# The order of two jobs of VectorE in the attention loop: normalising a result, and making the low parts of a prepared piece

## The chip, the cores and the metric

The kernel runs on one core of one Trainium2 chip. The metric is the time of one execution on the device, in microseconds (us); the figure of a kernel is the median of its runs. TensorE does the matrix products, VectorE, ScalarE and GpSimd the rest, and SyncE issues most of the DMA transfers. An engine does its instructions in the order of the program, and a semaphore is how one waits for another.

## The reference

One step of a decoder layer for a prompt of 1024 positions and for 8 single sample tokens, 1024 wide. Cut to what matters here, for each head of the prompt:

```python
z = rmsnorm(x, g) @ w_in                       # then q, k, v of each head, q and k normalised per head
sc = einsum('bqhe,bkhe->bhqk', q, k) * scale + bias    # causal; the bias is a decay or a position bias
p = softmax(sc)
o = einsum('bhqk,bkhe->bqhe', p, v)
```

There are four heads of forgetting attention (A), four of cross-attention into 256 memory tokens (M), and four of dilated attention (C). Each sample token attends to 4096 cached keys and values, which lie in pages that a table names (A), and to smaller caches (C, M). The outputs go through a norm and `w_out`, and then comes a ConvFFN with `w_up` and `w_down`.

## The kernel before

Products are made nearly exact by splitting an operand into a high part (a rounded copy, type fp32r) and a low part (the value less its high part). There are three stages one after the other: the projections, the attention loop, and the output projection with the ConvFFN.

**The attention loop** has 80 steps `g`, `H, s = divmod(g, 8)`: ten units `H` of eight steps. `H` 0 to 3 are the heads of A, 4 and 5 are M (two heads at a time), 6 to 9 are C. In A and C a step makes 128 queries against all the keys before them, and the query tiles alternate between long and short (`ALTERNATE = [7, 0, 6, 1, 5, 2, 4, 3]`): an even step has 8, 7, 6 or 5 blocks of 128 keys, an odd step 1, 2, 3 or 4. In M each step has 4 blocks. H = 9 takes the tiles from 7 down to 0. The loop is unrolled by hand on each engine, and the order of an engine's calls in a step is the order of its queue.

- **TensorE**, step g: `tp(g-2)`, the transposes of the weights of softmax (L1098, L1103); `prep`, the transposes of a piece of q or k of the next unit into bank 3 of PSUM (L983); `qk(g)`, the scores (L1082, L1083, in M L1089, L1090); `v_sum`, a product for the sample tokens (L1139) that uses a 512 KB gather of cached values; `pv_(g-3)`, weights times values (L1116, in M L1120).
- **ScalarE**, step g: a copy of transposed weights (`eva`, L1532), `hi` (the high part of a prepared piece), `ex(g)` (the exponentials, L1521).
- **VectorE**, step g: `evb(g-2)`, the copy of transposed weights beyond four blocks (L2198, even steps of A and C); `score(g)`, scores out of PSUM with the bias and their maximum (L2185, in M L2190); `lo`, the low part of the piece that TensorE transposed one step earlier (L2146 or L2150 for a unit of A or C, two of L2136 or L2140 for a unit of M); `k_mul` in odd steps to g = 31 (L1902) and `k_sum` in the step behind (L1910), which make the samples' scores out of a 512 KB tile of cached keys; `out(g-3)`, a reciprocal (L2207, in M L2214) and the product that writes the normalised result to `oN` (L2210, in M L2217); then the odd jobs, among them `cm_dot` (L2227 and L2229).

**The pieces.** A unit of A or C is prepared in four pieces, at steps s = 0, 2, 4, 6 of the unit ahead of it, a unit of M in three, at s = 0, 3, 6. VectorE makes the low part one step later, so for A and C in odd steps. From g = 3 on there are 33 steps with `lo`: 27 for a unit of A or C, 6 for one of M.

**Who waits for what.** `out(g-3)` waits for `pv_(g-3)`, which TensorE issues last in its own step g. `pv_(g-3)` waits for `out(g-4)`, since all results use the same bank:

```python
def pv_(g):
    ...
    T_.wait("s_o", g)            # out(g - 1) is done with bank 6
def prep(H, piece):
    ...
    T_.wait("p_lo", PN[(H, piece)] - 1)      # the piece before has left bank 3
def out(g):
    T_.wait("s_pv", g + 1)
```

`score(g)` waits for `qk(g)`, `qk(g)` for `score(g-2)`, `tp(g)` for `ex(g)`. SyncE loads key tiles by `k_load`, each when `k_sum` has freed its slot, and at its step 29, behind one of these, it loads `qdil` (1 MB, into a part of `oN`), for which the first `cm_dot`, at g = 35, waits.

Of the kernel before, what the change touches and what calls it, by code (L numbers as in the profile page):

```python
# [98 lines left out]
def build(nc, t):  # L99
# [5 lines left out]
    with ctx:  # L105
# [205 lines left out]
        def S(name):  # L311
            if name not in sems:
                sems[name] = ctx.enter_context(nc.semaphore(name))
            return sems[name]
# [160 lines left out]
        def two(H):  # L475
            return HEADS[H][0] != MEMG

        def prep_piece(H, s):

            if H + 1 >= len(HEADS):  # L480
                return None
            return (PREP_TWO if two(H + 1) else PREP_MEM).get(s)
# [8 lines left out]
        def qtile(g):  # L491
            H, s = divmod(g, NT)
            return s if not two(H) else ALTERNATE[s] if H + 1 < len(HEADS) else NT - 1 - s
# [32 lines left out]
        def k_total(n):  # L526
            return 64 * (n // 4 + 1) if n < NKA else 64 * (NKA // 4) + 16 * ((n - NKA) // 4 + 1)
# [1289 lines left out]
        def _(dve):  # L1817
# [81 lines left out]
            def k_mul(n):  # L1899

                kv = ring[:, n % 4]
                dve.tensor_tensor(kv, kv, qb[:, n // 8:n // 8 + 1, :].broadcast_to([P, 4, WG]), ALU.mult).then_inc(S("dve_chain"), 1)  # L1902
                chain[0] += 1
                multiplied[n] = chain[0]

            def k_sum(n):

                kv = ring[:, n % 4]
                out = sA[:, n // 8, 4 * (n % 8):4 * (n % 8) + 4, :]
                dve.tensor_reduce(out=out, in_=kv.rearrange("p g (h e) -> p (g h) e", e=HD), axis=AX.X, op=ALU.add)\  # L1910
                    .then_inc(S("k_used"), 1)
# [93 lines left out]
            def column_max(i):  # L2005

                grp, a, b, bank_, c0 = GMAX[i]
                T_.wait("mx_pe", 2 * i + 1)
                link(dve.tensor_reduce(out=mx[0:b - a], in_=ps[0:b - a, bank_, c0:c0 + P], axis=AX.X, op=ALU.max))
                dve.tensor_scalar(mxb[0:b - a, :], ones[0:b - a, :], mx[0:b - a], None, ALU.mult).then_inc(S("mx"), 1)  # L2010
# [158 lines left out]
            def score(g):  # L2169

                H, s = divmod(g, NT)
                grp, hh = HEADS[H]
                W = P * nblk(g)
                T_.wait("s_qk", g + 1)
                if two(H):
                    if grp == ATT:
                        T_.wait("toeA_ld", 16)
                        bias_ = toeA[:, 0:W][:, ::-1]
                    else:
                        T_.wait(f"toeC_ld{hh % 2}", 16 * (hh // 2 + 1))  # L2180
                        bias_ = toeC[:, hh % 2, 0:W][:, ::-1]
                    if g >= 2:
                        T_.wait("s_tpa", g - 1)
                        T_.wait("s_tpb", big_to[g - 1])
                    dve.tensor_tensor_reduce(out=lg[:, g % 2, 0:W], in0=SBANK(g % 2)[:, 0:W], in1=bias_, scale=-1.0,  # L2185
                                             scalar=3.0e38, op0=ALU.add, op1=ALU.min, accum_out=nm[:, g % 2, 0:1])\
                        .then_inc(S("s_nm"), 1)
                else:
                    T_.wait("s_exp", g - 1)
                    dve.tensor_reduce(out=nm[:, g % 2, 1:3], in_=SBANK(g % 2)[:, 0:W].rearrange("p (a c) -> p a c", a=2), axis=AX.X,  # L2190
                                      op=ALU.max, negate=True).then_inc(S("s_nm"), 1)

            def evb(g):
                nb = nblk(g)
                if nb > 4:
                    T_.wait("s_tpb", big_to[g + 1])
                    T_.wait("s_pv", g - 1)
                    dve.tensor_copy(pts[:, g % 2, 4:nb, :].rearrange("p b c -> p (b c)"),  # L2198
                                    ps[:, 5, 0:(nb - 4) * P]).then_inc(S("s_evb"), 1)

            def out(g):
                grp, hh = HEADS[g // NT]
                T_.wait("s_pv", g + 1)
                col = OCOL[grp] + hh * HD
                if two(g // NT):
                    one, o0 = ((0, 1), (HD, 0))[(g // NT) % 2]
                    dve.reciprocal(rc[:, g % 2, 0:1], ps[:, 6, one:one + 1]).then_inc(S("dve_chain"), 1)  # L2207
                    chain[0] += 1
                    T_.wait("dve_chain", chain[0])
                    dve.tensor_scalar(oN[:, qtile(g), col:col + HD], ps[:, 6, o0:o0 + HD], rc[:, g % 2, 0:1],  # L2210
                                      None, ALU.mult).then_inc(S("s_o"), 1)
                else:
                    z = ps[:, 6, 1:1 + 2 * HD].rearrange("p (a e) -> p a e", a=2)
                    dve.reciprocal(rc[:, g % 2, :], ps[:, 6, 0:2 * HD + 2:2 * HD + 1]).then_inc(S("dve_chain"), 1)  # L2214
                    chain[0] += 1
                    T_.wait("dve_chain", chain[0])
                    dve.tensor_tensor(oN[:, qtile(g), col:col + 2 * HD].rearrange("p (a e) -> p a e", a=2), z,  # L2217
                                      rc[:, g % 2, :].unsqueeze(2).broadcast_to([P, 2, HD]), ALU.mult).then_inc(S("s_o"), 1)
# [91 lines left out]
            for g in range(STEPS + 3):  # L2310
                H, s = divmod(g, NT)
                if 0 <= g - 2 < STEPS:
                    evb(g - 2)
                if g < STEPS:
                    score(g)
                piece = prep_piece(*divmod(g - 1, NT)) if g else None
                if piece:
                    lo((g - 1) // NT + 1, piece)
                if g in K_STEP:
                    n = K_STEP[g]  # L2320
                    T_.wait(f"ring_ld{n % 4}", k_total(n))
                    k_mul(n)
                if g - 1 in K_STEP:
                    n = K_STEP[g - 1]
                    T_.wait("dve_chain", multiplied[n])
                    k_sum(n)
                if g >= 3:
                    out(g - 3)
                if g in TURN_MAX:
                    column_max(TURN_MAX[g])  # L2330
                if g in SEND_MAX:
                    max_copy(SEND_MAX[g])
                if g == 2:
                    subtract_a(0)
                if g == 32:
                    forget_bias(1)
                    maxima(0, 4, 8)
                if g == 35:
                    subtract_a(1)
                    new_weight(0)  # L2340
                if g in CMK_AT:
                    cm_dot(CMK_AT[g])
                if g == 45:
                    dil_bias()
                    new_key(1)
                    maxima(1, 0, 8)
                if g == 56:
                    T_.wait("k_used", NKA + NCM)
                    maxima(2, 0, 8)
                if g == 48:  # L2350
                    subtract_cm(1)
                    new_weight(1)
                if g == 60:
                    subtract_cm(2)
                if g == 54:
                    key_sums(0)
                if g == 55:
                    key_sums(1)
                if g == 63:
                    key_sums(2)  # L2360
                if g in (56, 57):
                    w_out(g - 56)
                if g == 59:
                    sample_gate()
                if 68 <= g < 76:
                    scale_early(g - 68)
                if g == STEPS - 3:
                    T_.wait("samp_pe", 1)
                    dve.tensor_copy(small[0:8, :, 148:152], ps[0:8, 7, 0:24].rearrange("p (g h) -> p g h", h=8)[:, :, 0:NH])\
                        .then_inc(S("den_cp"), 1)  # L2370
                if g == 75:
                    T_.wait("s_pv", 8 * NT)
                    w_out_lo(0)
                if g == STEPS - 2:
                    for x in range(2):
                        scale_last(x)
                if STEPS < g:
                    turn_lo(g - STEPS - 1)
# [461 lines left out]
```

## Time and profile before

| | |
|---|---|
| median of 3 runs | 1390.29 us (1386.17 to 1390.61) |
| the profiled execution, its time / its span | 1387.22 / 1385.5 us |
| busy over the span: TensorE, its weight loads | 1320.2 us (95%), 1208.8 us (87%) |
| busy over the span: VectorE, ScalarE, GpSimd | 960.5 (69%), 550.7 (40%), 250.7 us (18%) |
| mean granted clock of TensorE, share of full speed | 0.978 |
| HBM traffic over the span | 144 GB/s |

Busy time is that of instructions that work; waits are idle time. A granted clock of 1.00 is 2.4 GHz, 0.50 is 1.2 GHz. The attention loop runs from about 300 to 569 us of the span; behind it TensorE has the output projection and the ConvFFN to do, which take the rest.

### The profile page before, as it was taken

The numbers are of one execution on the slowest core, as the hardware profiler recorded it, in microseconds if no ns is written. First come the engines' busy times: TensorE is split into PE (matmuls) and PEld (weight loads), VectorE is DVE, ScalarE is ACT, GpSimd is POOL, SyncE is SP. The second block draws the span as 40 slices with busy tenths as digits, with TensorE's granted clock in tenths as the row PEclk, the third lists the DMA queues.
The fourth block names the chain that finished last, engine by engine and source line by source line (L and its number), as shares of the span: only waits on it lengthen the run. The fifth ranks groups of instructions, "written<-read, shape, count | busy, mean of one in ns | idle before, by whom it ended". The sixth has DMA issues, their size and how long they took to land.

```text
span 1385.5 us, 24359 instructions
## 1 busy us (share of the span) xinstructions
PE 1320.2 (95%) x9293; PEld 1208.8 (87%) x9293; DVE 960.5 (69%) x1391; ACT 550.7 (40%) x908; POOL 250.7 (18%) x242
## 2 busy tenths in 40 slices
PE   6899999989988899899999999999999999999999
PEld 4668788866767677899899999999999999999999
DVE  6848789979987777758868878778878896111111
ACT  6422221146656566543544434543443454100100
POOL 5540013342332251100101111110110100000000
PEclk9799999989998899999999999999999999999999
DMA  8148866669999865432132222222222185322222
GB/s 291 57 133 258 228 194 194 196 190 265 297 293 281 266 223 140 147 123 77 62 107 69 70 92 70 69 93 80 66 85 92 47 305 162 112 75 80 81 73 73
DMA packets 149613, 201.57 MB, mean 145 GB/s; under 512 B 12692, under 2 KB 112556, under 8 KB 149216
## 3 DMA queue, kind: packets, MB, share of 16 engines
q1 hardware_dynamic: 130684, 140.12, 33.1%
q0 software_dynamic: 12848, 46.73, 10.7%
q10 hardware_dynamic: 5964, 13.16, 3.2%
q8 instruction: 74, 1.21, 0.4%
q14 instruction: 43, 0.35, 0.1%
HBM read 169.64 MB, written 29.82 MB: 144 GB/s over the span
## 4 chain that ended last, share of the span: by engine, by line
PE 64%; DVE 14%; DMA 8%; issue 5%; POOL 3%; ACT 2%; ACTq 1%; SPq 1%; DVEq 0%; POOLq 0%
PE ps L1275 8%; PE ps L1276 8%; PE ps L1277 8%; PE ps L1336 5%; PE ps L1337 5%; PE ps L1338 5%; PE ps L1116 3%; PE ps L1015 3%; PE ps L1016 3%; PE ps L1017 3%; DMA upr<-in_w_upL 2%; PE ps L1139 2%; DMA vring<-in_cache_a_v,gtab 2%; DMA oN<-scr_qs 2%; PE ps L1098 2%
## 5 line engine op out<-in xcount | busy, mean ns | idle before, releaser
L1275 PE MATMUL ps<-hhi,uph 128*128 128x258 f32 x704 | 200.8, 285 | 4.5 <-issue 1.4
L1276 PE MATMUL ps<-hlo,uph 128*128 128x258 f32 x704 | 199.4, 283 | 0.0
L1277 PE MATMUL ps<-hhi,upl 128*128 128x258 f32 x704 | 199.1, 283 | 0.0
L1015 PE MATMUL ps<-whi,hhi 128*128 128x512 f32 (+1 forms) x376 | 145.9, 388 | 13.1 <-DVE wlo L1858 9.3
L2580 DVE TENSOR_TENSOR dnl<-dnr,dnh 128x896 fp32r<-128x896 f32 (+2 forms) x24 | 27.2, 1135 | 174.9 <-ACT dnh L1771 174.9
L1017 PE MATMUL ps<-whi,hlo 128*128 128x512 f32 (+1 forms) x376 | 142.7, 379 | 0.0
L1016 PE MATMUL ps<-wlo,hhi 128*128 128x512 f32 (+1 forms) x376 | 142.6, 379 | 0.0
L1275 PEld LDWEIGHTS ps<-hhi,uph 128*128 128x128 f32 x704 | 133.8, 190 | 6.4 <-DVE ug L2538 2.5
L1276 PEld LDWEIGHTS ps<-hlo,uph 128*128 128x128 f32 x704 | 134.0, 190 | 0.0
L1277 PEld LDWEIGHTS ps<-hhi,upl 128*128 128x128 f32 x704 | 133.6, 190 | 0.0
L2765 POOL TENSOR_TENSOR upr<-upr 128x512 f32<-128x512 f32 x22 | 30.3, 1375 | 450.3 <-DMA upr<-in_w_upL 373.7
L1336 PE MATMUL ps<-fh,dnh 128*128 128x344 f32 x336 | 107.5, 320 | 1.6 <-DVE dnl L2580 1.6
L1337 PE MATMUL ps<-fl,dnh 128*128 128x344 f32 x336 | 107.8, 321 | 0.0
L1338 PE MATMUL ps<-fh,dnl 128*128 128x344 f32 x336 | 107.2, 319 | 0.0
L1771 ACT ACTIVATE dnh<-dnr 128x896 fp32r<-128x896 f32 (+2 forms) x24 | 23.7, 987 | 192.8 <-DMA dnr<-in_w_down 192.8
L1015 PEld LDWEIGHTS ps<-whi,hhi 128*128 128x128 f32 x376 | 72.4, 193 | 31.0 <-DVE wlo L1858 12.6
L1116 PEld LDWEIGHTS ps<-vst,pts 128*128 128x128 f32 x576 | 69.4, 191 | 31.5 <-issue 27.5
L1655 ACT ACTIVATE uph<-upr 128x1024 fp32r<-128x1024 f32 (+1 forms) x66 | 79.3, 1203 | 40.6 <-DMA upr<-in_w_upL 38.0
L2467 DVE TENSOR_TENSOR upl<-upr,uph 128x1024 fp32r<-128x1024 f32 (+1 forms) x66 | 92.1, 1395 | 0.4 <-ACT uph L1655 0.3
L2730 POOL DMA_INDIRECT vring<-in_cache_a_v,gtab x64 | 63.5, 992 | 144.9 <-PE ps L1139 140.9
L1116 PE MATMUL ps<-vst,pts 128*128 128x65 f32 x576 | 76.3, 278 | 9.4 <-DVE oN L2210 6.6
L1017 PEld LDWEIGHTS ps<-whi,hlo 128*128 128x128 f32 x376 | 72.4, 192 | 13.9
(339 smaller groups left out, 3600.2 us busy)
## 6 DMA issues: line engine op xcount, KB each, us to landing
upr<-in_w_upL SPq DMA_DIRECT2D x88, 256.0 KB, 3.4
ring<-in_cache_a_k SPq DMA_DIRECT2D x168, 128.0 KB
scr_act<-va SPq DMA_DIRECT2D x22, 516.0 KB, 2.6
ring<-in_cache_a_k ACTq DMA_DIRECT2D x88, 128.0 KB
wst<-in_w_in SPq DMA_DIRECT2D x32, 256.0 KB, 3.7
fr<-scr_act SPq DMA_DIRECT2D x14, 516.0 KB, 5.5
dnr<-in_w_down SPq DMA_DIRECT2D x12, 448.0 KB, 3.9
dnr<-in_w_down SPq DMA_DIRECT2D x10, 512.0 KB, 4.0
```

Source lines behind the costliest of these rows:

```text
L1015: pe.matmul(out, lh, whi[:, sl, 0:w], start=(kc == 0), stop=False)
L1016: pe.matmul(out, lh, wlo[:, sl, 0:w], start=False, stop=False)
L1017: i = pe.matmul(out, ll, whi[:, sl, 0:w], start=False, stop=(kc == KC - 1))
L1116: i = pe.matmul(ps[:, 6, 0:HD + 1], pts[:, g % 2, j, :], vst[:, hp % 2, j, VCOL[H % 2]], start=(j == 0), stop=(j == nb - 1))
L1275: pe.matmul(out, hi_, r_hi[:, cs], start=(first and i == 0), stop=False, skip_group_check=not first)
L1276: pe.matmul(out, hi_, r_lo[:, cs], start=False, stop=False, skip_group_check=not first)
L1277: m = pe.matmul(out, lo_, r_hi[:, cs], start=False, stop=(i == 3), skip_group_check=not first)
L1336: pe.matmul(out, hi_, a_hi[:, cs], start=first, stop=False)
L1337: pe.matmul(out, hi_, a_lo[:, cs], start=False, stop=False)
L1338: m = pe.matmul(out, lo_, a_hi[:, cs], start=False, stop=last)
L1655: act.activation(uph[p % 2][:, a:b, :], upr[p % 2][:, a:b, :], ACT.Copy).then_inc(S("st_hi"), 1)
L2467: dve.tensor_tensor(upl[p % 2][:, a:b, :], upr[p % 2][:, a:b, :], uph[p % 2][:, a:b, :].bitcast(f32), ALU.subtract).then_inc(S("st_lo"), 1)
```

## The change

In a step that has a low part to make, VectorE calls `out(g-3)` straight behind `score(g)`, ahead of `lo` and so ahead of `k_mul` and `k_sum` too. In the other steps `out` stays where it was. No instruction is added or taken away.

```diff
                 if g < STEPS:
                     score(g)
                 piece = prep_piece(*divmod(g - 1, NT)) if g else None
+                if piece and g >= 3:
+                    out(g - 3)
                 if piece:
                     lo((g - 1) // NT + 1, piece)
                 if g in K_STEP:
                     n = K_STEP[g]
                     T_.wait(f"ring_ld{n % 4}", k_total(n))
                     k_mul(n)
                 if g - 1 in K_STEP:
                     n = K_STEP[g - 1]
                     T_.wait("dve_chain", multiplied[n])
                     k_sum(n)
-                if g >= 3:
+                if g >= 3 and not piece:
                     out(g - 3)
```

## Rows read from the trace of the kernel before

**Rows 1.** Windows: us, busy (count) PE, PEld, DVE, ACT, POOL, clock, DMA share, GB/s.
```profile
306.00:394.00 88.00, 80.52 (x701) 61.45 (x699) 78.83 (x169) 52.22 (x87) 28.05 (x27) 0.99 1.04 285
...
416.00:466.00 50.00, 42.65 (x306) 34.84 (x305) 37.55 (x77) 30.44 (x78) 8.85 (x10) 0.78 0.89 285
466.00:570.00 104.00, 98.22 (x891) 76.44 (x887) 78.17 (x201) 65.51 (x139) 33.31 (x39) 0.99 0.60 185
570.00:1385.50 815.50, 801.91 (x5930) 797.08 (x5930) 509.11 (x558) 292.48 (x394) 70.56 (x62) 1.00 0.29 96
```

**Rows 2.** Groups by line, 310 to 566 us: busy, mean ns | idle before.
```profile
L1116 PE MATMUL ps<-vst,pts 128*128 128x65 f32 x566 | 75.0, 278 | 8.7 <-DVE oN L2210 5.9 <-issue 2.2
...
L2146 DVE SCALAR_TENSOR_TENSOR qhl<-ps,ssx,qhl 64x512 fp32r<-64x512 f32 x14 | 10.5, 751 | 0.5
...
L2150 DVE TENSOR_TENSOR klc<-ps,khh 64x512 fp32r<-64x512 f32 x13 | 8.9, 685 | 0.2
```

**Rows 3.** VectorE in time, steps g = 8 to 10: start, us, instruction.
```profile
329.75 0.28 DVE L2210 TENSOR_SCALAR oN<-ps,rc 128x64 f32<-128x64 f32 x1
329.95 0.28 DVE L2185 CUSTOM_DVE_ANT_0 lg<-ps,toeA 128x128 f32<-128x128 f32 x1
...
330.16 0.68 DVE L2150 TENSOR_TENSOR klc<-ps,khh 64x512 fp32r<-64x512 f32 x1
330.76 1.21 DVE L1902 TENSOR_TENSOR ring<-ring,qb 128x1024 f32<-128x1024 f32 x1
331.89 0.15 DVE L2207 RECIPROCAL rc<-ps 128x1 f32<-128x1 f32 x1
332.08 0.28 DVE L2210 TENSOR_SCALAR oN<-ps,rc 128x64 f32<-128x64 f32 x1
332.40 0.69 DVE L2198 COPY pts<-ps 128x512 f32<-128x512 f32 x1
333.65 1.09 DVE L2185 CUSTOM_DVE_ANT_0 lg<-ps,toeA 128x896 f32<-128x896 f32 x1 [0.56 <-PE ps L1083]
```

**Rows 4.** TensorE in time, `pv_` of steps 9 and 11.
```profile
330.18 1.30 PE L1116 MATMUL ps<-vst,pts 128*128 128x65 f32 x10 [0.43 <-DVE oN L2210]
...
336.42 1.97 PE L1116 MATMUL ps<-vst,pts 128*128 128x65 f32 x16 [0.33 <-DVE oN L2210]
```

**Rows 5.** VectorE in time, steps 28 and 30.
```profile
390.81 1.51 DVE L2136 SCALAR_TENSOR_TENSOR qhl<-ps,ssx,qhl 64x512 fp32r<-64x512 f32 x2
...
397.76 0.83 DVE L2185 CUSTOM_DVE_ANT_0 lg<-ps,toeA 128x640 f32<-128x640 f32 x1 [0.65 <-PE ps L1083]
```

**Rows 6.** TensorE in time: its three long waits, and `pv_` at full clock.
```profile
394.24 1.75 PE L1116 MATMUL ps<-vst,pts 128*128 128x65 f32 x14 [2.49 <-DVE oN L2210]
...
421.28 1.97 PE L1120 MATMUL ps<-vst,pts 128*128 128x65 f32 x8 [3.57 <-DVE oN L2217]
...
435.03 1.10 PE L1120 MATMUL ps<-vst,pts 128*128 128x65 f32 x8
...
454.94 0.40 PE L1195 MATMUL ps<-ca,small 128*32 128x128 f32 x1 [2.31 <-DVEq L2003]
```

**Rows 7.** VectorE in time, steps 36 to 39.
```profile
420.94 0.29 DVE L2217 TENSOR_TENSOR oN<-ps,rc 128x128 f32<-128x128 f32 x1
...
431.06 0.69 DVE L2190 TENSOR_REDUCE nm<-ps 128x2 f32<-128x512 f32 x1 [3.11 <-PE ps L1090]
```

**Rows 8.** Windows: TensorE's clock (third from the end) behind two waits.
```profile
392.00:396.00 4.00, 1.76 (x16) 1.79 (x17) 3.60 (x7) 0.63 (x2) 0.95 (x1) 1.00 1.07 277
...
424.00:428.00 4.00, 4.00 (x25) 3.48 (x27) 3.19 (x5) 3.17 (x7) 0.00 (x0) 0.50 0.97 265
```

**Rows 9.** The chain that ended last: the load of `qdil`.
```profile
393.99 22.03 DMA oN<-scr_qs
```

**Rows 10.** VectorE in time, step 61 of head group C.
```profile
512.22 0.17 DVE L2207 RECIPROCAL rc<-ps 128x1 f32<-128x1 f32 x1 [1.34 <-PE ps L1116]
```

**Rows 11.** TensorE in time, `prep` of step 62.
```profile
512.68 0.60 PE L983 MATMUL ps<-ca,qst 128*128 128x128 f32 x4
```

## The prediction

> **What bounds the kernel now.** I read the page first (busy shares and the 40 slices), then the windows by stage, the groups by line in the attention loop, the three engines' instructions in time through the loop, and the chain that ended last. The windows give the shares [rows 1]: from 570 us on TensorE is busy 801.9 of 815.5 us, and the change has no instruction there, so whatever the loop gains or loses arrives whole at the end. The loop has three stretches. In the first, 306 to 394 us, VectorE is busy 78.8 of 88.0 us and TensorE 80.5: neither has room, and the DMA share is 1.04. In the second the granted clock averages 0.78, which is a mix of the full 2.4 GHz and 1.2 GHz. In the third TensorE is busy 98.2 of 104 us, VectorE 78.2.
>
> The instructions in time say how the two engines hang together in the first stretch. In an odd step the queue of VectorE has `score` (0.28 us long at g = 9), `lo`, `k_mul`, then `out` [rows 3]. The `pv_` for which that `out` waits started at 330.18, just behind the end at 330.03 of the `out` of the step before, and took 1.30 us [rows 4]. So `pv_` starts with `score`, and `lo` and `k_mul` (2 us together) fill the time in which it runs: by the time they end, at 331.97, the product is done and `out` goes at once. That is the fact on which I build. The `pv_` of an odd step belongs to an even, long tile: 8, 7, 6 or 5 blocks, 1.97 us for 8 and 1.30 for 5 [rows 4].
>
> **What could be gained.** An earlier `out` frees bank 6 for the next `pv_`. Over the 256 us of the loop the products of A and C waited 5.9 us for `out` [rows 2], most of it behind even steps, whose `out` the change doesn't move; the two waits of 0.43 and 0.33 us at steps 9 and 11 are of this kind [rows 4]. In an odd step the next `pv_` on TensorE comes only after transposes, a piece, long scores and a `v_sum`; it doesn't wait for the `out` that is moved. Two long waits are different, and I cost them below.
>
> **The change, first stretch.** It adds and removes no instruction. At g = 9 `out` now waits for the end of `pv_` at 331.48. From the rows: 0.05 us from there to the reciprocal, 0.39 until the next instruction (start to start), `lo` 0.60, `k_mul` 1.13, `evb` 0.64, all start to start. The next `score` can start at 331.48 + 2.81 = 334.29, and it started at 333.65 [rows 3]. The shift is 0.64 us, less than the 1.24 us of new idle time, since VectorE had waited 0.56 us for the scores there and that wait is swallowed. TensorE isn't the later of the two: its next piece began at 332.20 and now waits for `lo` until 332.5, which puts the end of its scores, 333.62, at 334.0. The next even step has `score`, `k_sum`, `out` without a gap, and the next `pv_` hangs on that `out`, so each shift is kept. The same sum for the odd steps g = 5 to 25 (11 steps, the `pv_` 1.97 to 1.30 us long, `lo` 0.60 or 0.78) gives 0.59 to 0.96 us each, and 1.25 at g = 25, where no wait for scores is there to swallow: together 8.9 us. At g = 3 `pv_` is long done, and nothing is lost. Bounds: nothing, if another resource sets the pace (below), and 11 times 1.24, so 13.6 us, if no old wait swallows anything.
>
> **Steps 28 and 31.** Step 28 is even, and its piece is two instructions, 1.51 us [rows 5]. Its `out` has a one-block `pv_` long done and stood behind `lo` and `k_sum`: 2.7 us. TensorE waited 2.49 us for it [rows 6]. Moved, it lets TensorE go on at 391.8 instead of 394.24, and `score` of step 30, which waited for TensorE until 397.76 [rows 5], starts when VectorE is ready, at 396.4: 1.4 us gained. Step 31 is odd again, 0.9 us lost. Together -0.5.
>
> **Second stretch, M.** Step 36: `out` ended at 421.23 behind a `lo` of 1.5 us [rows 7], and TensorE sat idle 3.57 us, to 421.28 [rows 6]. Moved, `out` ends at 419.6 and the idle time is 2.0 us. Behind that wait the clock was 0.50 [rows 8]; eight instructions of `pv_` took 1.97 us there and 1.10 at full clock [rows 6], a ratio of 0.56. VectorE waited 3.11 us at step 39 for scores of this slow time [rows 7]. The end of my bounds where the clock still falls is the earlier start alone, -1.5. If it stays up, the 9.8 us from 421.28 to 431.06 take 9.8 x 0.56 = 5.5: -4.3 (the 1.5 isn't added, since the `score` of step 37 stands behind `lo` as before). Which one? The nearest rows are a wait of 2.49 us behind which the clock stayed at full level, and one of 2.31 us behind which it fell (the mean of 0.78 has both drops in it) [rows 1, 6, 8]. The new wait is shorter than either; I take -4.3.
> The Trainium skill, "TensorE: Matmul & The Clock Gate", section "What's actually happening", says that the halved clock is the default and that activity lifts it. By that rule a shorter idle time favours the full clock, a sum of +9.9; if the clock fell nevertheless, the sum would be +12.7.
> Steps 41, 43 and 45 have `cm_dot` behind `out`, so a `lo` of 0.6 to 0.75 us now lies in front of it that had been done while `pv_` ran: +0.6, +0.4, +0.8. Steps 33 and 39 cancel to about 0.1. Without the clock: +1.9.
>
> **The 1 MB load** took 22.03 us and landed just as VectorE came to it [rows 9]. Its issue stands behind `k_sum` of step 28, 0.4 us later than before against the rest, and its user comes 0.5 us earlier: a wait of 0 to 1 us. I take 0, as the transfers have more time per step.
>
> **Third stretch, C.** Steps 49, 51 and 53 have `cm_dot` too, and VectorE sets the pace: +0.6, +0.6, +0.4. From step 57 on TensorE does. At 61 `out` came at 512.22, waiting 1.34 us for `pv_` with `lo` already done [rows 10]; now `lo` (0.74 us) starts at 512.63 and ends at 513.4, and the next `prep`, which began at 512.68 [rows 11], waits: +0.7. The same at 63 and 69: +0.9, +0.7. At 65 and 67 a `v_sum` behind `pv_` covers it, at 55, 57 and 59 `pv_` is done or `prep` is late anyway: 0. Together +3.9.
>
> **Sum.** 8.9 - 0.5 + 1.9 - 4.3 + 3.9 = +9.9 us on the 1387.2 us of the profiled execution: 1397.1. That execution is 3.1 us below the median of the runs, so I forecast 1400.
>
> **Rivals.**
> 1. As forecast, but the clock falls behind step 36 as before: +12.7, 1403. For it: the fall behind 2.31 us [rows 6]. Chance 0.22; the forecast has 0.42.
> 2. New idle time makes the clock fall once more elsewhere: one fall cost 4.3 us, so 1407. Against it: the new gaps are 0.4 to 1.1 us of TensorE at a time. Chance 0.08.
> 3. Not slower: the transfers set the pace of the first stretch. The DMA share is 1.04 there [rows 1]. If the gathers and key tiles let no step go sooner, the stalls of VectorE fall into time that it would have waited anyway: the 8.9 go, and what stays is +1.0, 1391. It decides where the shift per pair of steps, 0.6 to 1.0 us, is below the wait for a transfer; but before, neither engine waits more than some tenths for one, in few steps. A part of it (half of the 8.9) gives 1395.5. Chance 0.18 for both.
> 4. Faster: the pace of the first stretch is the transfers' as in rival 3, and the clock stays up behind the 2.31 us wait too, which takes another 4.3: 1.0 - 4.3 = -3.3, 1387, and 1385 if the stalls of the third stretch are swallowed by half. It decides where both falls of the clock go and the first stretch costs nothing. Chance 0.04.
> What is left, 0.06, is no change within the measurement for reasons that I don't see.
> The Trainium skill, the same page, section "Architectural detail: the array is 16× 32×32, not 1× 128×128", calls VectorE's queue a strict FIFO. By that rule nothing passes the waiting `out`, which is what the stall in the first sum is made of; a queue that let `lo` pass would give no shift at all, 1390.
>
> **Range and chances.** What a measurement here can tell from no change is about 0.3%, 4.2 us. Low end: half of the first term, less one us: 1394. High end: one more fall of the clock: 1407. Slower by over 0.3% (above 1394.5): the forecast, rivals 1 and 2, and part of 3: 0.80. Within: 0.15. Faster: 0.05.
>
> **What the profile after would show.** The reciprocals of odd steps wait 0.7 to 1.6 us for L1116 in the first stretch, where they hardly did; `lo` and `k_mul` start behind L2210; a unit of A takes 28 us instead of 25; VectorE's waits for L1083 shrink. The 2.49 us wait is gone, and the 3.57 is 2.0. At steps 62, 64 and 70 `prep` waits for `lo`. Each busy total stays. I am wrong if `pv_` of odd steps starts earlier than the `out` ahead of it ends, if scores wait for the gathers, or if the clock has another pattern than assumed.

## The result, and the profile after

| | before | after |
|---|---|---|
| median of the runs beside each other | 1390.45 us (6 runs, 1386.17 to 1395.60) | 1415.78 us (6 runs, 1412.59 to 1422.85) |
| the profiled execution, its time / its span | 1387.22 / 1385.5 us | 1415.53 / 1413.7 us |
| mean granted clock of TensorE | 0.978 | 0.967 |

The ratio is 1.0202, 95% interval 1.0179 to 1.0226: the change makes the kernel 2.0% slower. By this ratio it is some 28 us, as between the two profiled spans (28.2); the two medians of the table lie 25.3 us apart. The forecast was +9.9 us, and its range ended at 1407. The direction was right, and the size is over two and a half times what I forecast.

The page of the kernel after: busy us (share) xinstructions, and the granted clock in 40 slices.

```profile
PE 1336.2 (95%) x9293; PEld 1218.3 (86%) x9293; DVE 962.9 (68%) x1391; ACT 550.8 (39%) x908; POOL 248.7 (18%) x242
...
PEclk9799999989987899999999999999999999999999
```

VectorE's work is the same, 962.9 us against 960.5. TensorE's instructions are the same too, but its busy time grew by 16.0 us, 1320.2 to 1336.2: the same products took longer, at a lower clock. That is the first sign that idle time of VectorE isn't the whole story.

The windows by stage of the kernel after (clock third from the end); the bounds are those of [rows 1], moved with the work.

```profile
306.00:404.00 98.00, 83.70 (x716) 62.71 (x714) 77.83 (x168) 52.02 (x87) 25.58 (x27) 0.99 1.02 265
404.00:428.00 24.00, 21.24 (x152) 16.44 (x151) 17.64 (x39) 11.88 (x23) 5.69 (x6) 0.79 1.05 331
428.00:482.00 54.00, 45.03 (x307) 36.02 (x305) 38.30 (x78) 30.74 (x79) 8.52 (x9) 0.78 0.67 216
482.00:594.00 112.00, 103.93 (x906) 78.87 (x905) 78.75 (x206) 66.16 (x139) 34.58 (x38) 0.95 0.56 172
```

The first stretch takes about 98 us instead of 88, at the same clock of 0.99. In the others the clock tells more. A mean of 0.78 over 54 us that is a mix of 1.00 and 0.50 is 54 x 0.22 x 2 = 23.8 us at half speed; with the other two windows (24 x 0.21 x 2 and 112 x 0.05 x 2) the loop after 404 us has 45 us at 1.2 GHz. The same sum over [rows 1] gives 22 + 2 = 24 us before.

**Step 9, where I worked the sum out.** VectorE in time, kernel after: start, us, instruction, and in brackets the idle time before it.

```profile
332.03 0.28 DVE L2185 CUSTOM_DVE_ANT_0 lg<-ps,toeA 128x128 f32<-128x128 f32 x1
...
333.60 0.17 DVE L2207 RECIPROCAL rc<-ps 128x1 f32<-128x1 f32 x1 [1.28 <-PE ps L1116]
333.80 0.28 DVE L2210 TENSOR_SCALAR oN<-ps,rc 128x64 f32<-128x64 f32 x1
334.00 0.67 DVE L2150 TENSOR_TENSOR klc<-ps,khh 64x512 fp32r<-64x512 f32 x1
334.60 1.21 DVE L1902 TENSOR_TENSOR ring<-ring,qb 128x1024 f32<-128x1024 f32 x1
335.73 0.68 DVE L2198 COPY pts<-ps 128x512 f32<-128x512 f32 x1
336.33 1.07 DVE L2185 CUSTOM_DVE_ANT_0 lg<-ps,toeA 128x896 f32<-128x896 f32 x1
```

From `score` of step 9 to `score` of step 10 it is now 336.33 - 332.03 = 4.30 us; it was 333.65 - 329.95 = 3.70 [rows 3]. The shift is 0.60 us, and the forecast for this step was 0.64. The reciprocal waits 1.28 us for the product, then `lo` and `k_mul` come, and the wait for scores is gone.

**Where the time came.** The start of each `score(g)`, read in the two traces, after less before, in us:

| g | 5 | 8 | 14 | 20 | 26 | 30 | 32 | 35 | 38 | 41 | 46 | 49 | 56 | 64 | 79 |
|---|---|---|---|---|---|---|---|---|---|---|---|---|---|---|---|
| shift | -0.17 | 2.09 | 4.35 | 7.12 | 10.67 | 9.18 | 10.37 | 13.78 | 12.36 | 16.05 | 18.76 | 18.05 | 22.20 | 24.11 | 25.32 |

Here it stands beside the forecast, with the steps grouped as there:

| | forecast | measured |
|---|---|---|
| ahead of g = 5 | 0 | -0.2 |
| first stretch, g = 5 to 26 | +8.9 | +10.8 |
| steps 28 to 48 (28 and 31: -0.5, 36: -4.3, M steps: +1.9) | -2.9 | +7.4 |
| from g = 49 to the end of the loop | +3.9 | +7.3 |
| behind the loop | 0 | +2.9 |
| sum | +9.9 | +28.2 |

Most of the miss is in the line of steps 28 to 48, 10.3 us of 18. TensorE in time, kernel after: its waits over 1.5 us from step 31 on, and two close together at step 53.

```profile
413.18 0.41 PE L983 MATMUL ps<-ca,kst 128*128 128x128 f32 x2 [1.67 <-DVE q1c L2136]
...
433.38 1.26 PE L1120 MATMUL ps<-vst,pts 128*128 128x65 f32 x8 [1.91 <-DVE oN L2217]
...
447.19 0.63 PE L983 MATMUL ps<-ca,kst 128*128 128x128 f32 x4 [1.78 <-DVE q1c L2136]
...
473.70 0.28 PE L1195 MATMUL ps<-ca,small 128*32 128x128 f32 x1 [2.06 <-DVEq L2003]
...
500.77 1.75 PE L1116 MATMUL ps<-vst,pts 128*128 128x65 f32 x14 [0.94 <-DVE oN L2210]
503.32 1.04 PE L1139 MATMUL ps<-vring,sA 128*4 128x256 f32 x8 [0.80 <-ACT mkd L1540]
```

The stretch behind each of these waits (the last two together) in windows of 4 us, kernel after; the clock is third from the end.

```profile
416.00:420.00 4.00, 4.00 (x23) 2.92 (x23) 3.28 (x7) 0.68 (x2) 1.75 (x3) 0.50 1.19 262
437.00:441.00 4.00, 4.00 (x27) 3.23 (x29) 2.49 (x5) 2.95 (x7) 0.00 (x0) 0.50 0.33 91
450.00:454.00 4.00, 4.00 (x23) 2.95 (x22) 1.42 (x4) 1.93 (x6) 0.77 (x1) 0.50 0.85 241
478.00:482.00 4.00, 4.00 (x17) 3.46 (x15) 1.27 (x3) 1.78 (x3) 0.00 (x0) 0.50 0.54 135
504.00:508.00 4.00, 4.00 (x22) 3.30 (x22) 2.85 (x4) 1.86 (x3) 1.26 (x1) 0.50 0.42 126
```

Behind all of them the clock stands at 0.50, 1.2 GHz. Two of these five falls were there before, behind waits of 3.57 us (now 1.91) and 2.31 us (now 2.06) [rows 6]. Three weren't in the profile before: `prep` at step 32 waits 1.67 us and at step 40 1.78 us, both for `lo` of a memory unit, and at step 53 two waits come close together. The third may not be of the change: runs 1, 4, 10 and 12 below have the old order at step 53, waits of 0.83 to 0.85 and about 0.80 us there, and a fall behind them. The kernel before has these two waits too (0.85 and 0.80 us) and stayed at 1.00. The `lo` that `prep` waits for at step 32 is this one; VectorE in time, kernel after, step 31.

```profile
411.00 0.17 DVE L2207 RECIPROCAL rc<-ps 128x1 f32<-128x1 f32 x1 [1.10 <-PE ps L1116]
411.20 0.28 DVE L2210 TENSOR_SCALAR oN<-ps,rc 128x64 f32<-128x64 f32 x1
411.52 1.51 DVE L2136 SCALAR_TENSOR_TENSOR q1c<-ps,ssx,q1c 64x512 fp32r<-64x512 f32 x2
```

In step 31 VectorE first waits for the product of a long tile, and then makes a double low part of 1.51 us, not a single one of 0.7. TensorE has nothing to do until it is made.

### The profile page after: what moved, and what is told of

Its sections match the earlier page's. It is cut to its first block, busy times and chain, and to the rows that moved or that the text cites. A ratio compares the mean times of both kernels' runs of the same rounds, so it can differ in the third digit from the quotient of the medians.

```text
span 1413.7 us, 24359 instructions
## 1 busy us (share of the span) xinstructions
PE 1336.2 (95%) x9293; PEld 1218.3 (86%) x9293; DVE 962.9 (68%) x1391; ACT 550.8 (39%) x908; POOL 248.7 (18%) x242
## 4 chain that ended last, share of the span: by engine, by line
PE 65%; DVE 17%; issue 5%; DMA 5%; POOL 3%; ACT 2%; ACTq 2%; SPq 1%; DVEq 0%; POOLq 0%
PE ps L1275 8%; PE ps L1276 8%; PE ps L1277 8%; PE ps L1336 5%; PE ps L1337 5%; PE ps L1338 5%; PE ps L1116 4%; PE ps L1015 3%; PE ps L1016 3%; PE ps L1017 3%; DMA upr<-in_w_upL 2%; PE ps L1139 2%; DVE ring L1902 1%; DVE lg L2185 1%; DVE sA L1910 1%
```

## The experiments

Each was timed against the kernel before on the same chip. "Shift" is the start of `score` less that of the kernel before, in the profiled executions. It is counted from g = 5 on, since executions differ in the steps ahead of that by up to 4 us whatever was edited: the clock from 310 to 318 us is 1.00 in the kernel before and 0.50 in runs 5 and 9.

**1 to 4. The change in four parts.** Each kernel has the new order in one group of steps alone:

```diff
+                early = bool(piece) and 3 <= g <= 27              # run 1
+                early = bool(piece) and 31 <= g <= 47 and g != 36 # run 2
+                early = bool(piece) and g >= 49                   # run 3
+                early = g in (28, 36)                             # run 4
+                if early:
+                    out(g - 3)
                 if piece:
                     lo((g - 1) // NT + 1, piece)
...
-                if g >= 3:
+                if g >= 3 and not early:
                     out(g - 3)
```

Run 1, the first stretch:

> Normalise first only in the odd steps 3 to 27 (13 steps; 12 of them have a piece), as before everywhere else. Theory (the result waits for its product and holds the low part and k_mul back): the score of step 28 starts 10.7 us later than before, as in the changed kernel, and that is kept to the end: +11 us, 1401. Rival A (most of the 25 us is halved clock, the stalls themselves are given back later): under +5. Rival B (transfers absorb it once the rest is as before): under +5, with new waits for gathers.

Run 2, the M steps and 31 without 36:

> Normalise first only in steps 31, 33, 39, 41, 43, 45 and 47. Theory (the next piece on TensorE waits for the late low part, the clock falls behind that wait, and everything in the fall takes nearly twice as long): +9 to +10 us, of which 2 to 4 are stalls of VectorE and the rest are two more falls of the clock than before, behind steps 31 and 39. Rival (the falls come from the slower pace ahead, not from these waits): +2 to +4 and the two falls of before.

Run 3, head group C:

> Normalise first only in the steps from 49 on. Theory (stalls of 0.5 to 1 us at steps 49, 51, 53, 61, 63 and 69, and a fall of the clock behind step 53): +5 to +7 us at the end of the loop. Rival (TensorE is the bound here and hides it): under +3.

Run 4, the two steps where a gain was forecast:

> Normalise first only in steps 28 and 36, where the product is done long before. Theory (TensorE no longer waits 2.5 and 3.6 us for the result): -1.4 at step 30 and -1.4 at step 38, so -3 us, or -6 if the clock stays up behind step 36. Rival (the steps behind are bound by something else and take it back): no change.

| run | median us | ratio to before (95%) |
|---|---|---|
| 1, first stretch | 1400.57 | 1.0075 (1.0050 to 1.0101) |
| 2, M | 1401.65 | 1.0083 (1.0058 to 1.0107) |
| 3, C | 1396.32 | 1.0040 (1.0019 to 1.0062) |
| 4, steps 28 and 36 | 1389.93 | 0.9996 (0.9981 to 1.0011) |

The four add up to 0.75 + 0.83 + 0.40 - 0.04 = 1.94%, the whole change is 2.02%: the parts hardly act on each other. In us these are 10.4, 11.5, 5.6 and -0.6; the forecast for the same steps was 8.9, 2.8, 3.9 and -5.7. So the timed runs, and not only one profile of each kernel, put the largest miss, 8.7 us, in the steps of run 2, and the next, 5.1 us, in steps 28 and 36. (The profiled execution of run 2, 1394.86 us, is the fastest of its six, and that of run 3, 1402.82, the second slowest of its ten.) In run 1 the shift grows from 2.99 at g = 5 to 13.85 at g = 26, +10.9, as in the whole change. In run 2 the shift is 0.2 at g = 30 and 9.4 at the end of the loop, where the forecast for its steps was 0.9 + 1.9 = 2.8: here is the error. TensorE in time, run 2, shows the same two new waits for `lo`, with step 36 left as it was:

```profile
404.21 0.66 PE L983 MATMUL ps<-ca,kst 128*128 128x128 f32 x2 [1.67 <-DVE q1c L2136]
...
424.36 1.97 PE L1120 MATMUL ps<-vst,pts 128*128 128x65 f32 x8 [3.58 <-DVE oN L2217]
437.49 0.66 PE L983 MATMUL ps<-ca,kst 128*128 128x128 f32 x4 [1.78 <-DVE q1c L2136]
```

Run 4 was to give the two gains alone, and gave nothing that can be measured. Its profile shows the gain at step 28, -1.4 us (2.94 at g = 28, 1.53 at g = 30), and then a loss of 3.1 at g = 36. VectorE in time and the chain that ended last, run 4:

```profile
421.19 1.23 DVE L2227 TENSOR_TENSOR ring<-ring,oN 128x1024 f32<-128x1024 f32 x1 [3.03 <-DMA oN<-scr_qs]
```

```profile
397.32 23.84 DMA oN<-scr_qs
```

This is the 1 MB load of `qdil`, for which I had taken 0 and bounded 0 to 1 us. It was issued 3.33 us later than in [rows 9] (that execution ran 2.94 us late at step 28, and `k_sum` behind `out` adds 0.4), and took 1.8 us longer, so it landed at 421.16. `score` of step 30 had won 1.4 us back by then, and `cm_dot` waited 3.03 us. The -1.4 of step 36 (5.10 to 3.70) and -1.8 at step 39 came after it, and the sum is nothing. That the early `out` makes this wait isn't shown: run 10 below has no early `out` and waits 3.00 us for the same load, run 12 has it and waits 1.89. In the whole change nothing waits for the load, since its steps take longer there.

**5 and 6. Which of the two jobs that `out` passed costs the time?** The order on VectorE was `out`, `lo`, `k_mul` in the change. Run 5 puts `out` between the two, run 6 puts `lo` last.

```diff
                 if piece:
                     lo((g - 1) // NT + 1, piece)
+                early = bool(piece) and g >= 3              # run 5: lo, out, k_mul / k_sum
+                if early:
+                    out(g - 3)
                 if g in K_STEP:
...
-                if g >= 3:
+                if g >= 3 and not early:
                     out(g - 3)
```

```diff
-                if piece:
+                if piece and g < 3:
                     lo((g - 1) // NT + 1, piece)
                 if g in K_STEP:
...
                 if g >= 3:
                     out(g - 3)
+                if piece and g >= 3:                        # run 6: k_mul / k_sum, out, lo
+                    lo((g - 1) // NT + 1, piece)
```

> In steps with a piece the order is low part, result, k_mul or k_sum: the low part is as early as before, the result is ahead of the multiply alone. Theory (what costs is the late low part everywhere, and the multiply held back in the first stretch): VectorE still fills part of the product's time with the low part, so the first stretch costs 2 to 4 us instead of 10.9; step 28 gives 1.4 or less back; from step 32 on it is the kernel before. 0 to +3 us. Rival (the wait for the product costs the same wherever it stands ahead of other work): +8 or more.

> The order is k_mul or k_sum, result, low part: the multiply fills the product's time, and the low part is the late one, as late as in the changed kernel or later. Theory for the first stretch (VectorE's idle time is the cost, the wait of TensorE for the low part is covered): +2 to +5 us at step 28. From step 31 on the order is that of the changed kernel, with the same late low parts: +12 to +15 at the end of the loop, of both together +15 to +19. Rival (the late low part is the whole cost in the first stretch too): +10 there, +25 in all.

| run | median us | ratio (95%) | shift over the first stretch, g = 5 to 26 |
|---|---|---|---|
| 5, `lo`, `out`, `k_mul` | 1388.11 | 0.9991 (0.9973 to 1.0010) | +1.0 |
| 6, `k_mul`, `out`, `lo` | 1407.00 | 1.0123 (1.0096 to 1.0150) | +8.7 |

Run 6 missed my theory by far. There `out` has `k_mul` ahead of it and hardly waits, so idle time of VectorE for `pv_` can't be the cause, yet the first stretch loses 8.7 us. The waits from 318 to 395 us say what took its place: engine and line, waited for: us, times, longest. First the kernel before:

```profile
DVE lg L2185 <- PE ps L1083: 4.1, 10, 0.6
```

The kernel after:

```profile
DVE rc L2207 <- PE ps L1116: 15.2, 11, 1.8
...
PE ps L983 <- DVE qhl L2146: 4.7, 6, 0.9
...
PE ps L983 <- DVE klc L2150: 1.6, 4, 0.5
```

Run 6:

```profile
DVE lg L2185 <- PE ps L1083: 11.7, 11, 1.4
DVE rc L2207 <- PE ps L1116: 2.3, 5, 0.7
...
PE ps L983 <- DVE qhl L2146: 4.7, 6, 0.9
...
PE ps L983 <- DVE klc L2150: 1.7, 4, 0.5
```

In run 6 `lo` is late, `prep` (L983) waits for it, the scores stand behind `prep` on TensorE, and VectorE waits 11.7 us for the scores. The change has the same waits on TensorE, 6.3 us (6.4 in run 6), hidden behind VectorE's own idle time. So there may be two limits that lie on each other. Runs 9 to 11 take `prep` out of the way to see.

Run 5 is the neutral place: `lo` comes on time, and `k_mul` behind `out` costs only 1.0 us. Over all of the loop it is no change within the measurement.

Run 6 shows one more thing. `prep` at step 32 waits 1.67 us for the double `lo`, as in the kernel after, but in this execution the clock stays up behind the wait (third from the end):

```profile
413.82 0.41 PE L983 MATMUL ps<-ca,kst 128*128 128x128 f32 x2 [1.67 <-DVE q1c L2136]
```

```profile
417.00:421.00 4.00, 3.83 (x38) 2.69 (x39) 3.63 (x9) 1.37 (x4) 1.41 (x2) 1.00 1.17 228
```

Steps 31 to 35 cost 0.35 us there (9.81 to 10.16) and 4.6 in the kernel after. So of what that step costs the wait itself is the small part, and the clock the large one.

**7 and 8. Is it the clock?** In both, TensorE multiplies the identity by itself into an unused part of PSUM where it would wait; nothing reads these products, and the rest is as in the kernel they are added to.

```diff
+            def keep_warm(bank_, n):
+                for _ in range(n):
+                    pe.matmul(ps[:, bank_, 0:P], ident, ident, start=True, stop=True)
...
+                if g in WARM_PREP:                # ahead of prep: run 8, {32: 10, 40: 11}
+                    slot_free(g)
+                    keep_warm(2 * (g % 2), WARM_PREP[g])
...
+                if g in WARM_PV:                  # ahead of pv_: run 7 {37: 20}, run 8 {37: 12}
+                    keep_warm(5, WARM_PV[g])
...
+                if g in WARM_MX:                  # ahead of L1195: run 7 {46: 14}, run 8 {46: 12}
+                    keep_warm(5, WARM_MX[g])
```

Run 7, on the kernel before:

> The kernel before, with 20 and 14 products of the identity (128x128, into bank 5 of PSUM, which nothing uses there; the outputs are the same) on TensorE at step 37 ahead of the product and at step 46 ahead of the transposed maxima, where it sat idle 3.6 and 2.3 us. Theory (the clock falls behind a stretch with little work, and the 10 us at 1.2 GHz behind each cost about 4): no fall behind these two, -4 to -8 us, 1384. Rival (the fall has another cause, or VectorE sets the pace there): no change, or +1 for the products themselves.

Run 8, on the kernel after:

> The changed kernel with 10, 12, 11 and 12 products of the identity on TensorE in its waits at steps 32, 37, 40 and 46 (banks of PSUM that are free there; the outputs are the same). Theory (its three extra falls of the clock in M come from these waits, which the late low part made): the score of step 48 starts 9 to 12 us later than in the kernel before instead of 18, and the whole is 6 to 9 us faster than the changed kernel, 1408. Rival (the falls follow the slower pace in general): as the changed kernel, 1416.

| run | median us | ratio to before (95%) |
|---|---|---|
| 7, before with products in its two long waits | 1382.31 | 0.9944 (0.9922 to 0.9967) |
| 8, after with products in its four | 1398.24 | 1.0067 (1.0035 to 1.0099) |

Windows from 400 to 490 us, in turn before, after, run 7 and run 8; the clock is third from the end.

```profile
400.00:490.00 90.00, 79.62 (x634) 62.71 (x631) 70.19 (x151) 54.35 (x133) 24.45 (x26) 0.87 0.88 273
```

```profile
400.00:490.00 90.00, 77.84 (x553) 60.24 (x555) 63.92 (x138) 48.06 (x113) 18.95 (x20) 0.79 0.77 245
```

```profile
400.00:490.00 90.00, 84.16 (x774) 66.85 (x766) 77.63 (x166) 57.81 (x142) 29.67 (x30) 1.00 0.94 290
```

```profile
400.00:490.00 90.00, 82.27 (x747) 66.53 (x745) 72.99 (x158) 54.97 (x132) 23.69 (x25) 1.00 0.85 275
```

From 404 us on the clock stays at 1.00 in both, and run 8 is 17.5 us faster than the change without the products, where I had expected 6 to 9. Some 8 us of that are the two falls that the kernel before has too, by run 7. (I had counted three extra falls in M; the profile after has two there, at steps 32 and 40.) TensorE in time, run 8, shows what fills the wait at step 32; ten calls are twenty records:

```profile
412.20 2.40 PE L1167 MATMUL ps<-ca 128*128 128x128 f32 x20
414.43 0.38 PE L983 MATMUL ps<-ca,kst 128*128 128x128 f32 x2
```

Now run 8 can be set against run 7, the new order against the old with no fall of the clock from 404 us to the last `score` in either. The difference of their shifts grows by 10.9 us over the first stretch, by 0.3 from g = 26 to 49, and by 5.4 in C (run 8: 0.64, 11.52, 4.73, 10.86 at g = 5, 26, 49, 79; run 7: 0.48, 0.51, -6.57, -5.88). One fall of run 7 lies just ahead, behind its wait for `out` at step 29, where it had no products:

```profile
394.99 1.75 PE L1116 MATMUL ps<-vst,pts 128*128 128x65 f32 x14 [2.49 <-DVE oN L2223]
```

```profile
396.00:400.00 4.00, 4.00 (x29) 3.34 (x28) 1.69 (x5) 1.97 (x3) 0.00 (x0) 0.63 1.03 268
```

It moved run 7 by 1.1 us (0.77 to 1.89, g = 28 to 30), so the 0.3 would be 1.4 without it. The steps from 28 to 48 then cost 0.3 to 1.4 us without the clock, and 6 to 7 of their 7.4 are the clock's; in C 1.9 of the 7.3 are. The timed runs agree: with products in both, the new order costs 1.0067 / 0.9944 = 1.0124, 17 us; the other 11 of the 28 are gone with the products.

**9 to 11. The two limits of the first stretch.** TensorE's `prep` moves behind the scores, so that a late `lo` holds up no score. Run 9 has it on the kernel after, run 10 on the kernel before as a control, run 11 on the order of run 6.

```diff
+                if g < STEPS:
+                    qk(g)
                 if piece:
                     prep(H + 1, piece)
-                if g < STEPS:
-                    qk(g)
```

> The changed kernel with the transposes of the next piece behind the scores on TensorE instead of ahead of them, so that no score waits for a late low part. Theory A (in the first stretch both VectorE's idle time and the late low part are enough by themselves, and each alone costs nearly the whole): still +8 to +10 at step 28 against step 5, and the waits of the piece move behind the scores; in M and C, where only the late low part counts, the extra falls of the clock go or move: 1403 to 1409. Rival B (the late low part is all of it): +1 to +3 in the first stretch and about 1393.

> The kernel before with the same move on TensorE, as the control of the run above. Both theories: within 4 us of the kernel before.

> Order k_mul, result, low part on VectorE, and the transposes of the piece behind the scores on TensorE: VectorE hardly waits and no score waits for the low part. Both theories: the 8.7 us of the same order without the move fall to +1 to +3 in the first stretch. If they stay, the late low part hurts in another way than by holding the scores.

| run | median us | ratio (95%) | shift, g = 5 to 26 |
|---|---|---|---|
| 9, `out`, `lo`, `k_mul`; `prep` late | 1404.85 | 1.0124 (1.0088 to 1.0161) | +10.5 |
| 10, as before; `prep` late | 1390.40 | 1.0008 (0.9980 to 1.0035) | +0.2 |
| 11, `k_mul`, `out`, `lo`; `prep` late | 1400.69 | 1.0077 (1.0054 to 1.0100) | +0.5 |

The waits of run 9 from 318 to 395 us:

```profile
DVE rc L2207 <- PE ps L1116: 15.4, 11, 1.8
```

The control shows that the move itself costs nothing. In the first stretch run 9 has no wait for `lo` among TensorE's products, and it loses 10.5 us all the same: VectorE's idle time alone, 15.4 us in 11 waits, is enough. Run 11 against run 6 shows the other: the same order on VectorE, +0.5 instead of +8.7, so there the loss was only the scores behind a late `prep`. Each limit alone costs 8.7 or 10.5 us, and both together 10.8. Run 11 is slower than before by 0.77% still; in its profile most of that comes in one place, where the shift goes from -3.0 at g = 31 to 5.2 at g = 35. There `k_mul` waited 4.10 us for its tile of cached keys (line 1), so that the double `lo` behind it came late, TensorE waited 5.31 us for it (line 2), and the clock fell. VectorE and TensorE in time, run 11:

```profile
401.80 1.23 DVE L1902 TENSOR_TENSOR ring<-ring,qb 128x1024 f32<-128x1024 f32 x1 [4.10 <-DMA ring<-in_cache_a_k]
...
405.12 0.66 PE L983 MATMUL ps<-ca,kst 128*128 128x128 f32 x2 [5.31 <-DVE q1c L2136]
```

**12. The best of what was seen.** The kernel before with `out` first only at steps 28 and 36, and products at steps 37 (12) and 46 (14).

> The kernel before with normalise first in steps 28 and 36 alone, and 12 and 14 products of the identity on TensorE at steps 37 and 46. Theory (the 1.4 us of step 30 come on top of the clock kept up): -7 to -11 us, 1381. Rival (the earlier result is worth nothing once the clock stays up): as the kernel before with the products, 0.994.

1382.95 us, ratio 0.9945 (0.9918 to 0.9973): the same as run 7. The early `out` adds nothing to it. In its profile `cm_dot` waited 1.9 us for the load of `qdil`, the wait at step 37 outlasted the twelve products by 1.16 us, and the clock fell behind it all the same (0.72 from 424 to 436 us). Run 7 is the simplest version that beats both kernels, by 0.56% and, as 0.9944 / 1.0202, by 2.5%.

## Why the prediction was wrong, point by point

Two steps of it failed. It let a late `lo` cost its own length on VectorE and nothing on TensorE, where the double `lo` of steps 31 and 39 made waits of 1.67 and 1.78 us with a fall of the clock behind them: forecast 2.8 us for the steps of run 2, measured 11.5. And it took the clock to stay up behind step 36, a gain of 4.3 us; with the 1.4 at step 28 that made 5.7, where run 4 measured 0.6.

- **First stretch, 8.9: the mechanism was right, the size low.** It measured 10.8 (10.9 in run 1). At the step that I worked out the shift is 0.60 against 0.64; over the pairs it is 0.6 to 1.3, where I had 0.6 to 1.0 and 1.25 for the last. The wait of TensorE's `prep` for `lo`, of which I had said that it isn't the later of the two, is nearly as late, and by run 6 would cost 8.7 by itself. The bound of 13.6 held.
- **Steps 28 and 31, -0.5.** The gain at 28 was forecast as 1.4, and `score` of step 30 came 1.4 us sooner (10.59 to 9.18). Step 31 was the first error. I priced its `lo` as one of 0.9 us of shift on VectorE, and didn't follow the double `lo` (1.51 us) to the one who waits for it. TensorE's `prep` at step 32 waited 1.67 us, the clock fell, and steps 31 to 35 cost 4.6 us.
- **Step 36, -4.3: this step of the prediction failed.** I held that the clock would stay up behind a wait of 2.0 us, since it had stayed up behind 2.49 us [rows 6]. The wait was 1.91 us, near the 2.0 that I worked out, and the clock fell, as it did behind this wait in all four executions that have it (after, runs 6, 9 and 11). What came was the end of my bounds where it falls: -1.4, against my -1.5. The row that I leaned on was the luck of one execution: the same wait of 2.49 us at step 29 had a fall behind it in runs 1 and 7. The page of the Trainium skill that I named, "TensorE: Matmul & The Clock Gate", section "What's actually happening", says that activity lifts a clock that is otherwise halved; the traces agree as far as runs 7 and 8 go, 1.00 from 400 to 490 us with products in the waits against 0.87 and 0.79 without. My reading of it, that a shorter wait would be safe, was wrong.
- **Rival 2, chance 0.08.** It is what came, at steps 32 and 40 by the new waits, and at step 53, where a fall comes with the old order too. I had argued against it that "the new gaps are 0.4 to 1.1 us of TensorE at a time"; that is true of the pieces for A and C (0.5 to 1.0 us), and false of the two double ones, 1.67 and 1.78. Nor is a gap in that range safe: at step 53 the clock fell behind 0.94 and 0.80 us. A row that I had [rows 5] shows a double `lo`, 1.51 us. Its `prep` was the next thing in TensorE's queue.
- **M steps, +1.9.** With the clock out of it, the steps from 28 to 48 come to +0.3 to +1.4 (run 8 less run 7), where the forecast without the clock is 0.9 - 1.4 - 1.5 + 1.9 = -0.1. With the clock they cost 7.4.
- **C, +3.9.** The clock-free part is 5.4, by run 8 less run 7: 2.4 from g = 49 to 56, where I had 1.6, and 3.1 behind it, where I had 2.3. The shifts at 62, 64 and 70 are there, 0.9, 1.0 and 0.9 for my 0.7, 0.9 and 0.7. The early ones are larger since `prep` waits for `lo` there too, 0.53 us at step 52 and 1.00 at step 56. The other 1.9 is the clock, which fell in step 53; since it falls there with the old order too, it isn't shown that the change made it.
- **Rivals 3 and 4, the transfers.** Wrong: the first stretch took the whole shift with a DMA share of 1.02, and no wait for a transfer appears in its list of waits. But the transfers aren't far off. Where a run keeps the pace of the kernel before through the first stretch, VectorE often waits for one at the end of it: 1.6 to 2.3 us for a key tile at step 27 in runs 2, 4, 7, 10 and 12, 2.02 and 4.10 us for one at step 31 in runs 3 and 11, and for `qdil` in runs 4, 10 and 12. With the slower first stretch (after, runs 1, 6, 8, 9) no such wait appears, nor in the profile of the kernel before.
- **VectorE's queue.** The Trainium skill, the same page, section "Architectural detail: the array is 16× 32×32, not 1× 128×128", calls it a strict FIFO, and the trace after agrees: `lo` starts only behind the reciprocal that waited, at 334.00 behind 333.60.

So of the 28.2 us, 10.9 + 0.3 + 5.4 = 16.6 are waits that VectorE's order makes, and 9.0 are the clock's in the loop (7.4 - 0.3 and 7.3 - 5.4); with the fall of run 7 at step 29 taken out it is 17.7 and 7.9. The timed runs say 17 and 11. The forecast had 12.7 for the first and -2.8 for the second.

**What stays open.** The 2.9 us behind the loop: in the profiles of the twelve experiments this part differs from that of the kernel before by -1.8 to +2.6 us, whatever was edited, so it may be the scatter of one execution; no run tells it apart. Why the clock stays up behind a wait in one execution and falls behind the same wait in another isn't settled either, and with it the share of each fall: in steps 28 to 48, with the old order in all of them, the shift changed by -4.1 us in run 1 and, with the old order to step 48, by +7.0 in run 3.

## What to carry to other kernels

When an instruction is moved back in a queue, ask who on the other engines waits for it and for how long, at every size that it comes in: the longest form of it, not the mean, makes the worst wait. An instruction that waits for a product belongs behind work that fills the time of that product, and a job that feeds another engine belongs ahead of it; the order `lo`, `out`, `k_mul` lost nothing, each of the other two lost over 1%. And where TensorE has to wait 1 to 2 us or more, look at the clock behind the wait, in several executions, and try some products that nobody reads in it.

## What the runs showed of the hardware that I had not expected

The granted clock fell to 0.50 behind waits of TensorE of 1.67, 1.78 and 1.91 us, and stood at 1.00 behind one of 2.49 us [rows 6, 8]; the length of a single wait doesn't decide. Nor does the code: in the profiled executions the same wait is followed by a fall in some and not in others.

| TensorE waits | us | clock fell in | stayed at 1.00 in |
|---|---|---|---|
| step 29, old order at 28 | 2.49, 2.50 | runs 1, 7 | before, run 2 |
| step 32, `lo` late | 1.67 | after, run 2 | run 6 |
| step 37, `out` first at 36 | 1.91 | after, runs 6, 9, 11 | none |
| step 40, `lo` late | 1.78 | after, runs 2, 6 | none |
| step 53, old order | 0.83 to 0.85, 0.80 or 0.81 | runs 1, 4, 10, 12 | before, runs 5, 7 |
| step 53, new order | 0.94, 0.80 | after, runs 3, 6 | run 8 |

Ten to twenty products of the identity in a wait kept it up in runs 7 and 8; in run 12, where the wait outlasted twelve of them, it fell. How long it stays down differs too. Run 1 has the order of the kernel before in all steps from 28 on, and its window from 400 to 490 us reads:

```profile
400.00:490.00 90.00, 77.02 (x647) 62.14 (x647) 71.41 (x155) 54.86 (x131) 22.43 (x24) 0.92 0.90 282
```

0.92 against 0.87, so 90 x 0.08 x 2 = 14 us at half speed against 23, although it holds a third fall, the one behind 2.49 us. In run 3, with the old order up to step 48, VectorE waited 2.02 us for a key tile at step 31, TensorE 2.24 us where it had waited 0.25 before, the clock fell, and the shift went from 0.9 to 7.8 us by g = 36, to stay there. One profile therefore isn't enough to say what the clock does in a kernel, and a forecast that rests on one row of it rests on luck; the ratios of the timed runs carry the argument.
